# The scan's skip term moves from VectorE to TensorE's accumulation, the sum of squares of the grouped norm to ScalarE

## The chip, the cores and the metric

The kernel runs on one core of a Trainium2 chip. The metric is the device time of the program in microseconds, the median of the runs. The engines are TensorE (PE in the profile; PEld its weight loads), VectorE (DVE), ScalarE (ACT), GpSimd (POOL, which here issues the row gathers) and SyncE (SP, which issues the loads of weights).

## The reference

A decoder layer on 1024 tokens of width 1024. One projection gives the inputs of a pooling mixer, of a Mamba-2 mixer and of two gates; the gated sum goes through an output projection and a LayerNorm, then through a retrieval over 16384 experts and another LayerNorm. The part that matters here is the Mamba-2 mixer:

```python
def ssm_mixer(z, xbc, dt_raw, conv_w, conv_b, dt_bias, a_log, d_skip, norm_w, out_w):
    xbc = jax.nn.silu(causal_depthwise_conv(xbc, conv_w, conv_b))
    ...
    y = ssd_scan(xs, dt, a, bm, cm)
    y = y + d_skip.astype(jnp.float32)[:, None] * xs.astype(jnp.float32)
    y = y.reshape(b, l, SSM_INNER) * jax.nn.silu(z.astype(jnp.float32))
    yg = y.reshape(b, l, SSM_GROUPS, SSM_NORM_GROUP)
    yg = yg * lax.rsqrt(jnp.mean(yg * yg, axis=-1, keepdims=True) + RMS_EPS)
    y = (yg.reshape(b, l, SSM_INNER) * norm_w.astype(jnp.float32)).astype(z.dtype)
    return y @ out_w
```

There are 32 heads of 64 channels in 8 groups of 4 heads (256 channels), a state of 128, and chunks of 128 tokens. The retrieval takes for each token the 128 best of the experts (8 heads, 16 each), a dot product of the token with each expert's row `expert_u[i]`, and a weighted sum of the rows `expert_v[i]`.

## The kernel before

Tokens lie on the 128 partitions for the retrieval; one *pair* is one expert of each of 128 tokens: a gather of 128 rows of 4 KB from `eu` and one from `ev` (for the last 224 of the 1024 pairs one gather of both). VectorE does the dot product (L1498) and, for a part of the pairs, the weighted sum (L1524); the other pairs are summed by TensorE, with a diagonal that ScalarE makes (L929, L621). The rows go through 12 buffers.

The layer ahead of the retrieval runs in five superchunks c of 1, 1, 2, 2 and 2 chunks of 128 tokens. Each superchunk has a stage A of four blocks j (512 channels of x, 2 groups each), then the output pairs (`front_pair`), the output projection with LayerNorm (`front_w`) and the queries and top 16 (`front_d`). The retrieval of the tokens of superchunk c runs beside the layer of superchunk c + 1. Nothing schedules that at run time: every engine has its instructions in an order written out by hand, where `until(p)` puts in the pairs up to number p, and `weave(p, front, steps)` spreads the steps of a generator (each ends at a `yield`) over the pairs up to p. In a block j the scan takes the places 20 to 32 of 32. WIDTHS says how many pairs go with stage A: in superchunk 0 none, in 1 ten a block, in 2 twenty-two, in 3 thirty-one, in 4 thirty-two. While superchunk 0 runs there are no gathers. In superchunks 0 to 2 VectorE does the causal convolution (L1269, L1271), in 3 and 4 TensorE does (L606).

In a block, TensorE projects seven blocks of weights (`front_a1`, L541, L549), turns x, B and C (`front_a2`), and then does the scan steps s, two for each chunk (gg is the group): `scan_scores` (L574, L577) gives the decays' exponents, ScalarE exponentiates them (`decays`, L1037), VectorE multiplies them with C B (`scan_pre`, L1299, signal `m_done`), and `scan_outputs` makes in the bank `ybank` the part from the old state (L589, right half) and the part from the chunk (L592, left half), and in `stbank` the new state's part (L596). The scores of step s + 1 stand before the outputs of step s, and block 7 of the weights (L549) after the outputs of step 0. From step 2 on, the outputs wait for `st_used`, VectorE's state sum of the step before (L1322).

VectorE's `scan_post` then takes the skip product d_skip x (L1310), waits for the outputs (`y_ready`), scales them (L1314), decays the state (L1317), adds the left half (L1320), adds the state's part (L1322), and after a `yield` adds the skip product (L1325), multiplies by silu(z) (L1330) and sums the squares (L1332). After the last step `rms_scale` makes mean + eps (L1338, `rms_in`), ScalarE takes the root (L1051), VectorE the reciprocal (L1341) and ScalarE scales y (L1055), on which TensorE turns y after the first two blocks of weights of the next block j (L709).

## Time and profile before

| what | value |
|---|---|
| time, median of 3 runs | 3943.45 us (3943.39 to 3955.12) |
| span of the profiled execution | 3897.3 us |
| its own time less its span, taken by the median | 46.2 us |
| TensorE busy | 3100.4 us, 80% |
| VectorE busy | 3040.1 us, 78% |
| ScalarE busy | 948.3 us, 24% |
| GpSimd busy | 2136.5 us, 55% |
| gathers and loads | 1394.76 MB, 358 GB/s in the mean |

The profile is one execution. Busy time is the time in which an engine worked on an instruction; issuing and waiting are not in it. The span goes from the first instruction to the last; what a run's time has beyond it lies before and after. In the rows below, a timeline has a start, a duration, the engine, the line of the kernel, the operation, what it writes and reads, and in brackets the engine's idle time just before, with what ended it. A matrix product in float32 has two instructions. "Granted clock" is the share of TensorE's full clock.

### The profile page before, as it was taken

The numbers are of one execution on the slowest core, as the hardware profiler recorded it, in microseconds if no ns is written. First come the engines' busy times: TensorE is split into PE (matmuls) and PEld (weight loads), VectorE is DVE, ScalarE is ACT, GpSimd is POOL, SyncE is SP. The second block draws the span as 40 slices with busy tenths as digits, with TensorE's granted clock in tenths as the row PEclk, the third lists the DMA queues.
The fourth block names the chain that finished last, engine by engine and source line by source line (L and its number), as shares of the span: only waits on it lengthen the run. The fifth ranks groups of instructions, "written<-read, shape, count | busy, mean of one in ns | idle before, by whom it ended". The sixth has DMA issues, their size and how long they took to land.

```text
span 3897.3 us, 43102 instructions
## 1 busy us (share of the span) xinstructions
PE 3100.4 (80%) x13336; PEld 2246.3 (58%) x13336; DVE 3040.1 (78%) x8238; ACT 948.3 (24%) x2282; POOL 2136.5 (55%) x1839
## 2 busy tenths in 40 slices
PE   8983888878789788999998879989878875565665
PEld 8873776567677456777775427777665422121221
DVE  4438975999985799888877988888877986677667
ACT  4411432123321213334312114333312110011111
POOL 0004543465554567766656677676656677555553
PEclk9997988989899999999999899999989897787877
DMA  6668999899888999999999999999999899999997
GB/s 240 210 230 304 377 363 352 319 347 353 312 330 334 335 357 363 400 383 385 381 410 380 351 356 405 379 389 362 375 386 392 305 351 352 423 423 422 424 423 332
DMA packets 316564, 1394.76 MB, mean 358 GB/s; under 512 B 35376, under 2 KB 40880, under 8 KB 251824
## 3 DMA queue, kind: packets, MB, share of 16 engines
q0 software_dynamic: 262656, 1073.86, 71.5%
q1 hardware_dynamic: 52384, 313.43, 20.6%
q10 hardware_dynamic: 1296, 4.72, 0.3%
q8 instruction: 108, 1.77, 0.2%
q14 instruction: 120, 0.98, 0.1%
HBM read 1387.67 MB, written 4.19 MB: 357 GB/s over the span
## 4 chain that ended last, share of the span: by engine, by line
DMA 15%; PE 15%; DVE 11%; POOL 7%; issue 6%; DVEq 2%; ACT 1%; another core or an unknown queue 0%; ACTq 0%; POOLq 0%
PE main L541 6%; POOL rowbuf L501 5%; DMA rowbuf<-euv,idx 4%; DVE rowbuf L1498 3%; DMA rowbuf<-ev,idx 3%; DVE acc L1524 2%; DMA ring<-euv,idx 2%; DMA xT<-euv,idx 2%; PE vbank L621 2%; PE turn L606 2%; DMA rowbuf<-eu,idx 2%; DMA late<-euv,idx 2%; PE main L549 1%; PE main L744 1%; DVE late L1464 1%
## 5 line engine op out<-in xcount | busy, mean ns | idle before, releaser
L501 POOL DMA_INDIRECT rowbuf<-eu,idx x800 | 964.5, 1206 | 989.8 <-DVE hdot L1498 520.8
L1498 DVE CUSTOM_DVE_ANT_0 rowbuf<-rowbuf,hb 128x1024 f32<-128x1024 f32 x884 | 1077.5, 1220 | 175.1 <-DMA rowbuf<-eu,idx 79.4
L501 POOL DMA_INDIRECT rowbuf<-ev,idx x800 | 885.5, 1107 | 453.9 <-issue 217.7
L621 PE MATMUL vbank<-rowbuf,vdiag 128*128 128x512 f32 x1436 | 770.8, 674 | 273.4 <-DMA rowbuf<-ev,idx 191.3
L541 PE MATMUL main<-xT,ring 128*128 128x256 f32 (+1 forms) x4480 | 810.4, 342 | 59.5 <-ACT mm L973 49.0
L541 PEld LDWEIGHTS main<-xT,ring 128*128 128x128 f32 x4480 | 729.2, 195 | 138.0 <-issue 67.0
L1524 DVE SCALAR_TENSOR_TENSOR acc<-rowbuf,hact,acc 128x1024 f32<-128x1024 f32 x525 | 674.8, 1285 | 85.6 <-DMA rowbuf<-ev,idx 63.4
L621 PEld LDWEIGHTS vbank<-rowbuf,vdiag 128*128 128x128 f32 x1436 | 284.3, 212 | 684.7 <-issue 531.5
L929 ACT ACTIVATE vdiag<-ident,hact 128x128 f32<-128x128 f32 x441 | 160.2, 395 | 464.1 <-DVE hact L1507 339.1
L729 PE MATMUL main<-late,ring 128*128 128x256 f32 (+1 forms) x1280 | 235.8, 347 | 32.9 <-issue 23.5
L729 PEld LDWEIGHTS main<-late,ring 128*128 128x128 f32 x1280 | 210.0, 198 | 58.1 <-issue 27.1
L541 PE MATMUL main<-early,ring 128*128 128x256 f32 (+1 forms) x1280 | 231.7, 340 | 0.7 <-ACT early L1099 0.7
L549 PE MATMUL main<-ring,xT 128*128 128x256 f32 x1024 | 228.9, 380 | 2.2 <-issue 2.1
L541 PEld LDWEIGHTS main<-early,ring 128*128 128x128 f32 x1280 | 207.9, 194 | 36.6 <-issue 16.8
L549 PEld LDWEIGHTS main<-ring,xT 128*128 128x128 f32 x1024 | 194.0, 190 | 29.9 <-issue 4.0
L1464 DVE SCALAR_TENSOR_TENSOR late<-iota,late,merged 128x50 f32<-128x50 f32 x1024 | 206.3, 265 | 1.2
L516 POOL DMA_INDIRECT rowbuf<-euv,idx x84 | 107.5, 1280 | 97.5 <-DVE acc L1524 75.8
L744 PE MATMUL main<-ring,merged 128*128 128x256 f32 x512 | 117.1, 390 | 29.5 <-DVE merged L1362 29.5
L621 PE MATMUL vbank<-ring,vdiag 128*128 128x512 f32 x128 | 85.9, 818 | 66.4 <-ACT vdiag L929 64.0
L589 PE MATMUL ybank<-state,CT 128*128 128x256 f32 x128 | 49.0, 470 | 100.9 <-issue 93.2
L744 PEld LDWEIGHTS main<-ring,merged 128*128 128x128 f32 x512 | 100.1, 196 | 47.4 <-DVE merged L1362 31.1
L1360 DVE TENSOR_TENSOR mm<-mm,lexp 128x512 f32<-128x512 f32 (+1 forms) x20 | 11.6, 582 | 145.4 <-ACT mm L1080 145.4
(223 smaller groups left out, 3667.2 us busy)
## 6 DMA issues: line engine op xcount, KB each, us to landing
ring<-wblocks SPq DMA_DIRECT2D x280, 1024.0 KB
rowbuf<-eu,idx POOLq DMA_INDIRECT x800
rowbuf<-ev,idx POOLq DMA_INDIRECT x800
pw<-poolw SPq DMA_DIRECT2D x20, 256.0 KB
h_out<-acc ACTq DMA_DIRECT2D x8, 512.0 KB
xT<-xt SPq DMA_DIRECT2D x3, 1024.0 KB, 17.0
zy<-x SPq DMA_DIRECT2D x3, 1024.0 KB
craw_ln<-ln1g SPq DMA_DIRECT2D x5, 512.0 KB
```

The source lines that it names most:

```text
L501: pool.indirect_dma_start(rows[r], None, (eu, ev)[table], bass.IndirectOffsetOnAxis(ap=idx[c % 2][:, u, k:k + 1], axis=0)).then_inc(row_re ...
L516: pool.indirect_dma_start(both[r], None, euv, bass.IndirectOffsetOnAxis(ap=idx[c % 2][:, u, k:k + 1], axis=0)).then_inc(both_ready[r], 16)
L541: last = pe.matmul(dst_[:, ct * tc:(ct + 1) * tc], w[:, k, ct * P:(ct + 1) * P], src[:, k, 0:tc], start=(k == 0), stop=(k == KD - 1))
L549: last = pe.matmul(dst_[:, t * 256:(t + 1) * 256], src[:, k, t * P:(t + 1) * P], w[:, k, :], start=(k == 0), stop=(k == KD - 1))
L606: last = pe.matmul(dst_[:, ct * tc:(ct + 1) * tc], cdiag[:, ct, k, :], craw[:, n % 2, ct, k:k + tc], start=(k == 0), stop=(k == TAPS - 1))
L621: last = pe.matmul(vbank[half][:, :], vdiag[:, n % DIAGS, :], r[:, half * 512:(half + 1) * 512], start=first, stop=False, skip_group_check ...
L729: last = pe.matmul(dst_[:, ct * tc:(ct + 1) * tc], (lo, hi)[k // KD][:, k % KD, ct * P:(ct + 1) * P], yT[:, k, 0:tc], start=(k == 0), stop ...
L744: last = pe.matmul(dst_[:, n * 256:(n + 1) * 256], merged[:, k, t * P:(t + 1) * P], w[:, k, :], start=(k == 0), stop=(k == KD - 1))
L929: act.activation(vdiag[:, n % DIAGS, :], ident[:, :], ACT.Copy, scale=hact[:, g % 2, q % TOPK:q % TOPK + 1]).then_inc(vdiag_ready, 1)
L1464: dve.scalar_tensor_tensor(out=sel1[:, k, :], in0=iota[:, :], scalar=posf[:, u, k:k + 1], in1=candi[:, u, :], op0=ALU.is_equal, op1=ALU.mu ...
L1498: last = dve.tensor_tensor_reduce(r, r, hb[c % 2][:, t, :], 1.0, 0.0, ALU.mult, ALU.add, hdot[:, g % 2, k:k + 1])
L1524: dve.scalar_tensor_tensor(out=a, in0=r, scalar=hact[:, g % 2, k:k + 1], in1=a, op0=ALU.mult, op1=ALU.add).then_inc(row_free, 1)
```

## The change

The skip term is no longer computed by VectorE. ScalarE makes, once a block j, four diagonal matrices 128x128 (`ddiag`) from the identity and a column of d_skip, now laid out by channel (`dsk`, 128x16). In `scan_outputs` TensorE multiplies x, as it stands by channels (`xs`), with two of them, into the left half of `ybank`. The bank is now one accumulation group: the first product starts it, and the skip products and the four products of the heads add to it. L1310 and L1325 go.

The squares are summed by ScalarE: an activation `Square` with the sum as a second output, one a scan step, its elements written to a part of `yT` that is free at the time. VectorE signals each gate product (`gated`). The root takes mean and eps as its scale and bias, so L1338 goes too.

```diff
+        dsk = sb("dsk", [P, INNER // P])
+        ddiag = sb("ddiag", [P, 4, P])
+        eps = sb("eps", [P, 1])
...
+                if s == 0:
+                    pe.wait_ge(ddiag_ready, c * AJ + j + 1)
                 pe.matmul(ybank[:, GW:2 * GW], CT[:, gg, t * P:(t + 1) * P],
-                          state[:, ds(j * 2 * GW + gg * GW, GW)], start=True, stop=True)
+                          state[:, ds(j * 2 * GW + gg * GW, GW)], start=True, stop=False, skip_group_check=True)
+                for ct in range(2):
+                    pe.matmul(ybank[:, ct * P:(ct + 1) * P], xs[:, 2 * gg + ct, t * P:(t + 1) * P],
+                              ddiag[:, 2 * gg + ct, :], start=False, stop=False, skip_group_check=True)
                 for h in range(HG):
                     last = pe.matmul(ybank[:, h * HD:(h + 1) * HD], mm[:, s % 2, h, :],
-                                     xd[:, s % 2, h * HD:(h + 1) * HD], start=True, stop=True)
+                                     xd[:, s % 2, h * HD:(h + 1) * HD], start=False, stop=(h == HG - 1),
+                                     skip_group_check=True)
...
                 conv_weights(c, j, 3)
+                for ct in range(4):
+                    last = act.activation(ddiag[:, ct, :], ident[:, :], ACT.Copy, scale=dsk[:, ds(j * 4 + ct, 1)])
+                last.then_inc(ddiag_ready, 1)
                 until(o(18))
...
                 until(o(30))
-                act.wait_ge(rms_in, c * AJ + j + 1)
-                act.activation(rms[:, 0:steps], rms[:, 0:steps], ACT.Sqrt).then_inc(rms_sqrt, 1)
+                for s in range(steps):
+                    act.wait_ge(gated, scans(c, j, s) + 1)
+                    act.activation(yT[:, j * 4 + s, 0:GW], yg[:, s // 2, (s % 2) * GW:(s % 2 + 1) * GW], ACT.Square,
+                                   accum_out=rms[:, s:s + 1])
+                act.drain()
+                act.activation(rms[:, 0:steps], rms[:, 0:steps], ACT.Sqrt, bias=eps[:, :], scale=1.0 / GW
+                               ).then_inc(rms_sqrt, 1)
...
                 dve.drain()
-                dve.tensor_tensor(yt2[:, :].rearrange("p (h d) -> p h d", h=HG), xv,
-                                  spread(dsk[:, ds(j * 2 * HG + gg * HG, HG)], HD), ALU.mult)
...
-                dve.tensor_tensor(yt1[:, :], yt1[:, :], yt2[:, :], ALU.add)
-                dve.drain()
...
-                dve.tensor_tensor(y, yt1[:, :], zs[:, t, gg * GW:(gg + 1) * GW], ALU.mult)
-                dve.drain()
-                dve.tensor_tensor_reduce(yt2[:, :], y, y, 1.0, 0.0, ALU.mult, ALU.add, rms[:, s:s + 1])
+                dve.tensor_tensor(y, yt1[:, :], zs[:, t, gg * GW:(gg + 1) * GW], ALU.mult).then_inc(gated, 1)
...
             def rms_scale(c, j):
-                dve.drain()
                 steps = 2 * CHUNK[c]
-                dve.tensor_scalar(rms[:, 0:steps], rms[:, 0:steps], 1.0 / GW, EPS, ALU.mult, ALU.add).then_inc(rms_in, 1)
                 yield
```

Three places in the engines' orders, all in superchunk 2. TensorE at the outputs of the last scan step of a block, before; `scr` is `xd`, `late` and `early` hold yT and x:

```order
L596 MATMUL stbank<-scr,btok 128x256 [waits st_used]
L589 MATMUL ybank<-state,CT 128x256 [waits st_used,y_free,m_done]
L592 MATMUL ybank<-scr,mm 128x64 x4
L596 MATMUL stbank<-scr,btok 128x256 [waits st_used]
L541 MATMUL main<-xT,ring 128x256 [waits main_free,w_ready0]
```

and now:

```order
L606 MATMUL stbank<-scr,btok 128x256 [waits st_used]
L595 MATMUL ybank<-state,CT 128x256 [waits st_used,y_free,m_done]
L598 MATMUL ybank<-ddiag,early 128x128 x2
L601 MATMUL ybank<-scr,mm 128x64 x4
L606 MATMUL stbank<-scr,btok 128x256 [waits st_used]
L545 MATMUL main<-xT,ring 128x256 [waits main_free,w_ready0]
```

Between the product with the state and those of the heads stand two more, with the diagonals (`early` holds `xs`).

VectorE from the last step's outputs to the reciprocal of the norm, before:

```order
L1320 TENSOR_TENSOR yt<-yt,ybank 128x256
L1322 TENSOR_TENSOR state<-state,stbank 128x256 [waits st_ready]
L1325 TENSOR_TENSOR yt<-yt 128x256
L1330 TENSOR_TENSOR zy<-yt,zy 128x256
L1332 ISA yt,rms<-zy 128x256
L1332 ISA rms 128x1
L1498 ISA rowbuf,hdot<-rowbuf,hb 128x1024 [waits row_ready6]
L1498 ISA hdot 128x1
L1524 SCALAR_TENSOR_TENSOR acc<-rowbuf,hact,acc 128x1024 [waits row_ready7,row_free]
L1338 TENSOR_SCALAR rms<-rms 128x4
L1341 RECIPROCAL rmsr<-rms 128x4 [waits rms_sqrt]
```

and now:

```order
L1332 TENSOR_TENSOR state<-state,cdec 128x256
L1335 TENSOR_TENSOR yt<-yt,ybank 128x256
L1337 TENSOR_TENSOR state<-state,stbank 128x256 [waits st_ready]
L1343 TENSOR_TENSOR zy<-yt,zy 128x256
L1507 ISA rowbuf,hdot<-rowbuf,hb 128x1024 [waits row_ready6]
L1507 ISA hdot 128x1
L1533 SCALAR_TENSOR_TENSOR acc<-rowbuf,hact,acc 128x1024 [waits row_ready7,row_free]
L1350 RECIPROCAL rmsr<-rms 128x4 [waits rms_sqrt]
```

The addition, the sum of squares and the scaling are gone; the row products (L1498 and L1524, now L1507 and L1533) stand between the gate product and the reciprocal as they did. The skip product, L1310, stood ahead of L1314 and is gone as well.

ScalarE from the last decays to the scaling of y (`zy` holds yg), before:

```order
L1037 ACTIVATE lexp<-main,nacum 128x128 [waits m_done,l_ready]
L1037 ACTIVATE lexp<-main,nacum 128x128 x3
L1051 ACT_TABLE_LOAD
L1051 ACTIVATE rms<-rms 128x4 [waits rms_in]
L1055 ACTIVATE zy<-zy,rmsr 128x256 [waits rms_rstd]
L1055 ACTIVATE zy<-zy,rmsr 128x256 x3
L973 COPY mm<-main 128x2x256 [waits block_done]
```

and now:

```order
L1050 ACTIVATE lexp<-main,nacum 128x128 [waits m_done,l_ready]
L1050 ACTIVATE lexp<-main,nacum 128x128 x3
L1065 ACTIVATE late,rms<-zy 128x256 [waits gated] x4
L1068 ACT_TABLE_LOAD
L1068 ACTIVATE rms<-rms,eps 128x4
L1073 ACTIVATE zy<-zy,rmsr 128x256 [waits rms_rstd]
L1073 ACTIVATE zy<-zy,rmsr 128x256 x3
L983 COPY mm<-main 128x2x256 [waits block_done]
```

The load of the root's table stood ahead of the wait for `rms_in`; it now stands behind the squares, which wait for `gated`.

## Rows read from the trace of the kernel before

**Rows 1.** Page, part 1: busy time, share of the span, instructions.
```profile
PE 3100.4 (80%) x13336; PEld 2246.3 (58%) x13336; DVE 3040.1 (78%) x8238; ACT 948.3 (24%) x2282; POOL 2136.5 (55%) x1839
```

**Rows 2.** Stretches: columns are in the first line; one block j each.
```profile
core 0: us, PE busy (x) PEld busy (x) DVE busy (x) ACT busy (x) POOL busy (x), PEclk, DMA share, GB/s
98.70:138.40 39.70, 38.84 (x295) 36.14 (x294) 21.23 (x66) 19.39 (x52) 0.00 (x0) 1.00 0.65 220
464.60:512.30 47.70, 41.98 (x290) 38.37 (x290) 43.88 (x94) 21.20 (x54) 25.69 (x21) 0.93 1.01 403
854.20:944.40 90.20, 79.45 (x377) 68.09 (x377) 85.71 (x155) 30.97 (x68) 55.99 (x45) 0.91 0.92 352
1718.00:1824.30 106.30, 100.07 (x467) 82.69 (x466) 90.01 (x147) 43.36 (x106) 71.76 (x62) 0.97 0.99 385
2360.00:2400.00 40.00, 40.00 (x187) 35.15 (x186) 29.51 (x39) 17.98 (x51) 29.80 (x26) 1.00 1.02 413
2457.30:2566.00 108.70, 100.79 (x472) 83.62 (x471) 91.82 (x150) 42.19 (x105) 73.56 (x65) 0.97 1.00 388
1810.90:1817.70 6.80, 4.61 (x14) 3.76 (x15) 6.26 (x16) 0.00 (x0) 4.54 (x4) 0.52 0.97 352
```

**Rows 3.** Timeline, VectorE, superchunk 3; in brackets the idle time before.
```profile
1784.41 0.69 DVE L1299 TENSOR_TENSOR mm<-lexp,cdiag 128x512 f32<-128x512 f32 x1 [2.94 <-ACT lexp L1037]
...
1798.74 0.69 DVE L1299 TENSOR_TENSOR mm<-lexp,cdiag 128x512 f32<-128x512 f32 x1 [1.12 <-ACT lexp L1037]
```

**Rows 4.** Timelines, TensorE, superchunk 2 (first row), then superchunk 3.
```profile
934.97 1.81 PE L592 MATMUL ybank<-scr,mm 128*128 128x64 f32 x8
...
1782.14 1.05 PE L577 MATMUL main<-upper,adtc 128*128 128x128 f32 x8
1783.03 1.02 PE L574 MATMUL main<-mask,ident 128*128 128x512 f32 x2
...
1813.10 1.19 PE L589 MATMUL ybank<-state,CT 128*128 128x256 f32 x2 [5.60 <-issue]
...
1819.05 13.11 PE L541 MATMUL main<-xT,ring 128*128 128x256 f32 x60
```

**Rows 5.** Timeline, VectorE, last scan steps of a block of superchunk 2.
```profile
933.80 0.41 DVE L1322 TENSOR_TENSOR state<-state,stbank 128x256 f32<-128x256 f32 x1
...
934.30 0.42 DVE L1325 TENSOR_TENSOR yt<-yt 128x256 f32<-128x256 f32 x1
...
935.69 1.22 DVE L1498 CUSTOM_DVE_ANT_0 rowbuf<-rowbuf,hb 128x1024 f32<-128x1024 f32 x1
...
938.21 0.42 DVE L1310 TENSOR_TENSOR yt<-early,dsk 128x256 f32<-128x256 f32 x1
938.55 0.42 DVE L1314 TENSOR_TENSOR yt<-ybank,eacum 128x256 f32<-128x256 f32 x1
...
944.12 0.17 DVE L1338 TENSOR_SCALAR rms<-rms 128x4 f32<-128x4 f32 x1
944.57 0.18 DVE L1341 RECIPROCAL rmsr<-rms 128x4 f32<-128x4 f32 x1 [0.27 <-ACT rms L1051]
```

**Rows 6.** Line L577: duration in ns, min/median/max, first and last start.
```profile
L577 PE MATMUL main<-upper,adtc x512: 272/275/421, 46.0 to 2764.6; 128*128 128x128 f32 x171
```

**Rows 7.** Timelines, ScalarE, superchunk 2, then eight diagonals of superchunk 4.
```profile
899.13 0.60 ACT L1000 ACTIVATE zy<-main 128x512 f32<-128x512 f32 x1 [3.75 <-PE main L549]
...
903.58 1.28 ACT L1037 ACT_TABLE_LOAD   x1
904.94 1.15 ACT L1037 ACTIVATE lexp<-main,nacum 128x128 f32<-128x128 f32 x4
...
944.33 0.20 ACT L1051 ACTIVATE rms<-rms 128x4 f32<-128x4 f32 x1 [20.79 <-DVE rms L1338]
944.78 1.71 ACT L1055 ACTIVATE zy<-zy,rmsr 128x256 f32<-128x256 f32 x4 [0.25 <-DVE rmsr L1341]
...
2716.84 2.44 ACT L884 ACTIVATE cdiag<-ident,cw 128x128 f32<-128x128 f32 x8
```

12 lines of the change are left out of this document (7 added, 5 removed).

## The prediction

> **What bounds the kernel now.** I read the page first: VectorE is busy 78% of the span and TensorE 80% [rows 1], so neither bounds the whole, and I went on by stage. The table of stretches has one row for one block j of each kind of superchunk [rows 2]. The block of superchunk 0 belongs to TensorE (38.84 of 39.70 us busy, VectorE 21.23). In superchunk 1 VectorE is busy 43.88 of 47.70 us while the DMA engines stand at share 1.01. In superchunk 2 it is VectorE: 85.71 of 90.20 us, and I take the rest for drains, since its timeline goes from one instruction to the next. In superchunks 3 and 4 it is TensorE: 100.07 of 106.30 us and 100.79 of 108.70. So time saved on VectorE counts fully in four of the twenty blocks and is bounded by something else in the others.
>
> In a block of superchunk 3 the two wait for each other. VectorE waits 2.94 us for the first decay product and 1.12 us for the third, both times for ScalarE's exponentials, which wait for TensorE's scores [rows 3]. TensorE waits once, 5.60 us before the outputs of the last scan step [rows 4], for the state that VectorE adds one step earlier. In the 6.8 us around the end of that wait its granted clock is 0.52 [rows 2], the lower of its two levels (1.2 of 2.4 GHz), and it leaves the scan 5.95 us after the wait.
>
> **What leaves VectorE.** In the timeline of superchunk 2 the skip product (L1310) starts 0.34 us before the next product (L1314) [rows 5]. From L1325 to the instruction behind the sum of squares is 935.69 - 934.30 = 1.39 us; of these three only the gate product stays, 0.35 us by the same spacing, so 1.04 us go. That is 0.34 + 1.04 = 1.38 us for each scan step. Once a block the scaling of the sums and the wait behind it go too: the reciprocal of superchunk 2 followed at 944.57 on L1338 at 944.12 [rows 5], 0.45 us.
>
> **What comes to TensorE.** Two products 128x128 by 128 columns a step. Nearest row: four of that shape, accumulated, from 1782.14 to 1783.03 [rows 4], 0.22 us each, so 0.44 to 0.46 us a step at the full clock (I take 0.46), and about 0.92 at the low one. Bounds: their whole recorded time, as if nothing overlapped, is four instructions (a product is two) of 275 ns [rows 6], 1.1 us a step; and it is 0 where TensorE waits anyway.
>
> **What comes to ScalarE.** Four diagonals a block: eight of the kind last 2.44 us [rows 7], so 1.2 us. They stand ahead of silu(z), before which ScalarE is idle 3.75 us in superchunk 2 [rows 7]: free, and if that cover were gone they would delay the copies of the turned blocks by 1.2 us. TensorE's new wait for them comes after four more steps of ScalarE, so it costs nothing. The squares: one 128x256 activation with a column as scale is 1.71/4 = 0.43 us [rows 7]. All but the last are done while ScalarE waits for the last gate (before, it stood 20.79 us idle there [rows 7]). Behind the last gate stand 0.43 (square), 1.28 (the table load, now after the squares, [rows 7]) and 0.20 (root): 1.9 us. VectorE has in that time, as the order shows, one pair of row products, 938.21 - 935.69 = 2.5 us [rows 5], so it does not wait. Queued behind the squares on ScalarE are the scaling of y and the copy of the pool block. They waited for the same last step before; there the root waited also for the pair of row products, so they start no later now. What the sum's read-out on ScalarE costs no row shows: between 0 and the 0.20 us of its smallest instruction, the root [rows 7]; I take 0, since the cover of 0.6 us holds either.
>
> The trace has a table load at 903.58 of 1.28 us and the exponential that needs it at 904.94 [rows 7], 0.08 us behind its end, so the load costs its own length. The Trainium skill, page "ScalarE: Activation LUTs", section "What ACT_TABLE_LOAD costs", adds a drain of about 1.38 us to each switch. The trace does not agree. By that rule the way behind the last gate would be 3.3 us; a mechanism of that size is rival D.
>
> **The sum by superchunk.**
> - Superchunk 0, four blocks, TensorE bound, two steps each: 8 x 0.46 = +3.7 us. VectorE's saving is worth nothing there.
> - Superchunk 1, four blocks: VectorE would save 2 x 1.38 + 0.45 = 3.2 us of each, but the block moves 403 GB/s x 47.70 us = 19.2 MB, and the fastest that a stretch of mixed traffic shows is 413 GB/s [rows 2]: 46.5 us. So -1.2 us a block: -5 us (0 to -6; without that floor -13).
> - Superchunk 2, four blocks: 4 x 1.38 + 0.45 = 5.97 us less. One new wait: from the state sum of step 2 (start 933.80) VectorE reaches the outputs of step 3 at 938.55 now [rows 5], and 0.34 + 1.04 us sooner then, 937.17; TensorE has them at 934.97 + 1.81 = 936.78 [rows 4], and with the two new products at the low clock at 937.70. So 0.53 us are given back: -5.44 a block, -21.8 us. The DMA floor is far (352 x 90.20 = 31.8 MB, 77 us at 413 GB/s).
> - Superchunks 3 and 4, eight blocks. TensorE's free time in a block is its one wait. What VectorE saves ahead of its third decay product is lost, as that waits for TensorE's scores (1.12 us already [rows 3]), and these come 0.46 later. After it VectorE saves 0.34 + 1.04 (step 1) + 0.34 (head of step 2) = 1.72, so the state for step 3 is there 1.72 - 0.46 = 1.26 us sooner. Then TensorE's way out: 5.95 us now, from 1813.10 to 1819.05 [rows 4]. Of these 4.6 us are at the low clock (to 1817.7 [rows 2]), worth 2.3 at the full one: 3.65 us of work, 4.11 with two more products. If the clock is low as long as now, it is 6.41 us and the block gains 1.26 - 0.46 = 0.8; if it does not fall, 4.11 us and 1.26 + 1.84 = 3.1. The wait shrinks from 5.60 to 5.60 - 3 x 0.46 - 1.26 = 3.0 us, so I take half of the low stretch of 6.8 us, 3.4: 4.11 + 1.7 = 5.81, a gain of 1.26 + 0.14 = 1.4. Eight blocks: -11.2 us (-6 to -25). What the last two steps save behind that point makes VectorE's wait at the next scan longer and nothing else.
>
> Sum: +3.7 - 5 - 21.8 - 11.2 = -34.3 us. The profiled execution has a span of 3897.3 us, so it becomes 3863.0; between a span and the median of 3943.45 lie 46.2 us that the change does not touch. Forecast: 3909.2 us, 0.9% faster. The stages behind the scans (output pairs, query, top 16, the last 224 pairs) keep their length.
>
> **Rivals.** (A) VectorE bounds everywhere from superchunk 1 on: 56 steps x 1.38 + 16 x 0.45 = 84 us less, plus 3.7: 3863 us. Against it: the waits of [rows 3] and the DMA share of 1.01.
> (B) Only superchunk 2 gains. In 3 and 4 VectorE, now faster, waits for rows from the DMA engines (shares 0.99 and 1.00 [rows 2]) and the state comes no sooner; TensorE pays 3 x 0.46 + 0.92 = 2.3 us a block, 18 us, and 3.7 in superchunk 0; superchunk 1 is held by the DMA engines. -21.8 + 18 + 3.7 = 0: 3943 us. For it: the same shares. Against: these are means, and in the scan part of superchunk 3 (1810.90) it is 0.97 at 352 GB/s.
> (C) Slower: the new products cost their whole recorded time, 1.1 us a step, in TensorE's path. Superchunks 0, 3 and 4 have 40 steps there: +44, and 8 of them at the low clock +9; the clock stays low as long as now; the state still comes 1.72 sooner in eight blocks, -14; superchunk 2 gains 5.97 less 1.8 of wait, -17, superchunk 1 -5. Together +17: 3960 us. It decides from about 0.8 us a step. Against it: the spacing of 0.22 us [rows 4], which is steady in a run of such products.
> (D) ScalarE's switch of tables, now behind the last gate, holds the root for as long again as the load itself, 2 x 1.28 us: the root is then 3.2 us behind the gate, against a cover of 2.5, and VectorE waits 0.7 us in each of the eight blocks of superchunks 1 and 2: +5.5, 3914.7 us. No row of this trace shows such a gap. This is the rule of the Trainium skill's page above, whose figure would make it +6.2.
>
> **How the numbers follow.** Forecast 0.64, A 0.07, B 0.13, C 0.08, D 0.08. The forecast's own range is 3892 (superchunk 1 at -6, 2 at -24, 3 and 4 at -25) to 3923 (0, -18, -6). The whole range goes from 3880, which leaves A out, to 3943, which takes in B and leaves out C. A measurement can tell about 0.3%, 12 us, from no change: faster by more is forecast, A, D: 0.79; within 0.3%: B and no more, 0.13; slower: C, 0.08.
>
> **What would show it.** Right: blocks of superchunk 2 at about 85 us instead of 90, with VectorE still without long waits but for half a microsecond at L1329; blocks of superchunk 3 at 104.9 instead of 106.3, with TensorE's wait before the last step's outputs at 3 us and a shorter low clock; VectorE's wait before the first decay product longer; the new products 0.22 us apart; ScalarE's root within 2 us of the last gate. Wrong: blocks of superchunk 0 longer than 40.6 us, VectorE waiting for y in every step, superchunk 3 unchanged or longer (B), or blocks there 5 us shorter (A).

## The result and the profile after

| | before | changed |
|---|---|---|
| median of six executions, us | 3943.4 (3926.2 to 3955.1) | 3909.4 (3898.2 to 3918.9) |
| ratio of the changed kernel to before | | 0.9907 [0.9877, 0.9936] |
| span of the profiled execution, us | 3897.3 | 3910.6 |

The changed kernel is 34.0 us faster, where 34.3 were forecast (3909.2 us). That the sum came out is luck: it hides two large errors that cancel. The stage that was to give most gave little, and the stage that was to give little gave most.

Read the last row of the table first. The time of an execution is its span and about 2 us (1.7 to 2.7 in the runs of this case; 3912.5 for the 3910.6 here). So there never were 46.2 us "between a span and the median": the profiled execution of before took some 3899 us, less than all six timed ones. Other chips ran before in 3879 to 3911 us (medians), and a timed execution can lie 20 us off its median in the kernel before and 26 us in the changed one (36.5 us in a variant below). The profile of the changed kernel is longer than the one of before although its median is lower. Two profiles can't be compared by their spans. They have to be compared piece by piece, and over several executions.

Page of the changed kernel, part 1, beside [rows 1]:

```profile
PE 3133.6 (80%) x13592; PEld 2271.8 (58%) x13592; DVE 2962.0 (76%) x7963; ACT 1002.9 (26%) x2490; POOL 2125.9 (54%) x1839
```

VectorE lost 78 us of work, TensorE got 33, ScalarE 55. Stretches of the changed kernel, with the columns of [rows 2]: one block j each of superchunks 0, 1, 2, 3 and 4, from reciprocal (L1350) to reciprocal; [rows 2] has its counterparts.

```profile
99.90:140.20 40.30, 39.44 (x300) 36.74 (x300) 18.61 (x57) 21.61 (x60) 0.00 (x0) 1.00 0.64 216
459.10:503.50 44.40, 41.01 (x300) 37.75 (x300) 41.26 (x86) 23.52 (x62) 26.62 (x21) 0.96 1.02 413
840.60:930.40 89.80, 82.14 (x401) 70.90 (x400) 80.75 (x139) 34.21 (x80) 55.07 (x45) 0.92 0.94 354
1598.30:1703.60 105.30, 100.01 (x473) 81.60 (x473) 84.17 (x129) 46.32 (x118) 73.81 (x62) 0.98 1.00 392
2454.30:2561.50 107.20, 101.95 (x485) 84.94 (x484) 86.90 (x133) 45.14 (x117) 72.57 (x62) 0.97 0.99 383
```

Superchunk 0 is 0.6 us longer (39.70 to 40.30), superchunk 1 is 3.3 shorter (47.70 to 44.40), superchunk 2 is 0.4 shorter (90.20 to 89.80) although VectorE works 5.0 us less in it. The stretch of superchunk 3 is that superchunk's first block here and its second in [rows 2]; first against first it is 1.3 shorter (106.6 to 105.3), while the second one is 3.3 longer here (106.3 to 109.6).

The whole span in pieces, each the time between two such reciprocals in a trace, means over two profiles of before and three of the changed kernel (two of them from the runs below, on other chips):

```
piece                                   before    changed   difference
start and first block                     61.5       59.8         -1.7
superchunk 0, next three blocks          118.2      120.9         +2.7
turn to superchunk 1, its first block    239.0      233.3         -5.7
superchunk 1, next three blocks          144.1      136.0         -8.1
turn to superchunk 2, its first block    294.0      290.4         -3.5
superchunk 2, next three blocks          283.4      280.5         -2.9
turn to superchunk 3, its first block    475.9      474.3         -1.5
superchunk 3, next three blocks          319.7      321.9         +2.2
turn to superchunk 4, its first block    524.7      519.5         -5.2
superchunk 4, next three blocks          337.4      333.3         -4.1
what stands behind the scans            1109.5     1108.6         -0.9
```

Superchunk 1 and the turns on both its sides hold 17 of the 29 us. From the second row to the sixth the two profiles of before and the three of the changed kernel don't overlap. From the turn to superchunk 3 on they do: the turn to superchunk 4 took 522.5 and 527.0 us before, and 513.3, 520.7 and 524.5 in the changed kernel. So the first and the last five differences can't be told from chance.

**Superchunk 1.** Here the forecast saw a floor of the DMA engines. TensorE's timelines show another bound. First before, then the changed kernel: the products that turn the normed y of the block before (L709, now L719), and the first 96 products of the projections behind them.

```profile
465.90 0.73 PE L709 MATMUL turn<-ident,zy 128*128 128x128 f32 x4 [2.56 <-ACT zy L1055]
466.42 12.49 PE L541 MATMUL main<-xT,ring 128*128 128x128 f32 x96
```
```profile
461.84 0.60 PE L719 MATMUL turn<-ident,zy 128*128 128x128 f32 x4
462.27 10.88 PE L545 MATMUL main<-xT,ring 128*128 128x128 f32 x96
```

Before, TensorE waited 2.56 us for ScalarE's scaled y, and the 96 products behind the wait took 12.49 us, with a granted clock of 0.87:

```profile
466.40:478.90 12.50, 12.50 (x100) 12.50 (x99) 10.92 (x25) 6.11 (x16) 6.52 (x7) 0.87 1.00 402
```

Now the y is there in time and the same products take 10.88. That is 2.56 + 1.61 = 4.17 us, less 2 x 0.44 for the new products: 3.3 us, which is what this block lost.

Other blocks lost more or less. Over all three blocks and all profiles the mean loss is 2.7 us: the first block lost about 4, the other two about 2. The wait is there in each of the twelve blocks of the four profiles with the old order of work (2.56 or 2.57 us), and in none of the changed kernel's. The low clock isn't always right behind it: in four of the twelve the 96 products took 10.88 us all the same. In three of these, of one profile, it comes later in the block, behind TensorE's wait for the turn of C (3.84 us in one), and the blocks are as long, 47.7 to 48.3 us. In the fourth, the second block of another profile, it comes less: the granted clock is 0.96 over a block of 46.7 us, where its neighbours have 0.90 and 48.9 and 48.8 us. In the changed kernel's first and second blocks it is 0.96 too. So the wait is worth 1.7 us net of the new products in every block, and the clock 1.6 us more in some. What else sets the later blocks is taken up behind the runs with one half each.

The scaled y comes sooner for two reasons. VectorE has less to do ahead of the last gate, and the root hangs on that gate instead of on the scaling (L1338) behind a pair of row products. The second reason in the timelines, before and then now:

```profile
508.65 0.42 DVE L1330 TENSOR_TENSOR zy<-yt,zy 128x256 f32<-128x256 f32 x1
...
512.06 0.17 DVE L1338 TENSOR_SCALAR rms<-rms 128x2 f32<-128x2 f32 x1
512.26 0.20 ACT L1051 ACTIVATE rms<-rms 128x2 f32<-128x2 f32 x1 [6.95 <-DVE rms L1338]
512.70 0.91 ACT L1055 ACTIVATE zy<-zy,rmsr 128x256 f32<-128x256 f32 x2 [0.23 <-DVE rmsr L1341]
```
```profile
501.45 0.42 ACT L1065 ACTIVATE late<-zy 128x256 f32<-128x256 f32 x1 [1.68 <-DVE zy L1343]
...
503.30 0.29 ACT L1068 ACTIVATE rms<-rms,eps 128x2 f32<-128x2 f32 x1
503.86 0.91 ACT L1073 ACTIVATE zy<-zy,rmsr 128x256 f32<-128x256 f32 x2 [0.27 <-DVE rmsr L1350]
```

From the start of the last gate to that of the scaling of y it was 4.05 us (508.65 to 512.70); now it is 2.87 (the gate starts at 500.99).

**Superchunk 2.** VectorE's timeline in the changed kernel (in brackets its idle time before; L1287 is the convolution's first operation, L1317 the decay product, L1329 the outputs):

```profile
861.28 0.62 DVE L1287 TENSOR_SCALAR early<-craw_ln,cw 128x256 f32<-128x256 f32 x2 [3.80 <-issue]
...
909.89 0.69 DVE L1317 TENSOR_TENSOR mm<-lexp,cdiag 128x512 f32<-128x512 f32 x1 [1.36 <-ACT lexp L1050]
...
926.20 0.42 DVE L1329 TENSOR_TENSOR yt<-ybank,eacum 128x256 f32<-128x256 f32 x1 [0.60 <-PE ybank L601]
...
927.88 0.43 DVE L1343 TENSOR_TENSOR zy<-yt,zy 128x256 f32<-128x256 f32 x1
...
930.56 0.17 DVE L1350 RECIPROCAL rmsr<-rms 128x4 f32<-128x4 f32 x1
```

VectorE's idle time in the block is 9.1 us (89.80 - 80.75), where it was 4.5 (90.20 - 85.71, [rows 2]). Before, no wait in it was over 0.8 us. The timeline has one more wait now, 1.08 us ahead of the second convolution, but the second profile of before has that one too (1.03). In the other two profiles of the changed kernel the first wait is shorter (2.40 us in one) and the block takes 88.4 and 88.5 us. Ahead of the 3.80 us ScalarE waits for TensorE's projection:

```profile
860.30 0.59 ACT L903 COPY craw_ln<-main 128x512 f32<-128x512 f32 x1 [5.73 <-PE main L545]
```

### The profile page after: what moved, and what is told of

It reads as the page before. It is cut to its first block, busy times and chain, and to the rows that moved or that the text cites. A ratio compares the mean times of both kernels' runs of the same rounds, so it can differ in the third digit from the quotient of the medians.

```text
span 3910.6 us, 43419 instructions
## 1 busy us (share of the span) xinstructions
PE 3133.6 (80%) x13592; PEld 2271.8 (58%) x13592; DVE 2962.0 (76%) x7963; ACT 1002.9 (26%) x2490; POOL 2125.9 (54%) x1839
## 4 chain that ended last, share of the span: by engine, by line
PE 26%; DMA 17%; DVE 16%; issue 8%; POOL 7%; DVEq 4%; ACT 2%; another core or an unknown queue 0%; ACTq 0%; POOLq 0%
PE main L545 11%; POOL rowbuf L505 6%; DMA rowbuf<-ev,idx 4%; DVE rowbuf L1507 4%; DMA rowbuf<-euv,idx 4%; PE main L553 3%; DVE acc L1533 3%; PE vbank L631 3%; PE turn L616 2%; DMA ring<-euv,idx 2%; DMA xT<-euv,idx 2%; DVE late L1473 2%; PE main L754 2%; PE main L739 2%; DVEq L1415 2%
## 5 line engine op out<-in xcount | busy, mean ns | idle before, releaser
L1507 DVE CUSTOM_DVE_ANT_0 rowbuf<-rowbuf,hb 128x1024 f32<-128x1024 f32 x884 | 1078.5, 1221 | 164.1 <-DMA rowbuf<-eu,idx 78.3
L545 PEld LDWEIGHTS main<-xT,ring 128*128 128x128 f32 x4480 | 721.0, 193 | 150.2 <-issue 80.4
L1533 DVE SCALAR_TENSOR_TENSOR acc<-rowbuf,hact,acc 128x1024 f32<-128x1024 f32 x525 | 675.5, 1287 | 81.9 <-DMA rowbuf<-ev,idx 62.3
L616 PE MATMUL turn<-craw_ln,cdiag 128*128 128x256 f32 x512 | 124.1, 393 | 16.0 <-issue 15.1
```

What stands on the lines that cost most here:

```text
L545: last = pe.matmul(dst_[:, ct * tc:(ct + 1) * tc], w[:, k, ct * P:(ct + 1) * P], src[:, k, 0:tc], start=(k == 0), stop=(k == KD - 1))
L616: last = pe.matmul(dst_[:, ct * tc:(ct + 1) * tc], cdiag[:, ct, k, :], craw[:, n % 2, ct, k:k + tc], start=(k == 0), stop=(k == TAPS - 1))
L1507: last = dve.tensor_tensor_reduce(r, r, hb[c % 2][:, t, :], 1.0, 0.0, ALU.mult, ALU.add, hdot[:, g % 2, k:k + 1])
L1533: dve.scalar_tensor_tensor(out=a, in0=r, scalar=hact[:, g % 2, k:k + 1], in1=a, op0=ALU.mult, op1=ALU.add).then_inc(row_free, 1)
```

## The experiments

My theory after the result: each stage had two bounds of nearly the same length, so what leaves one engine is worth something only until the other one binds. In superchunk 1 a wait of TensorE goes, whoever takes it away; in superchunk 2 TensorE's way through the projections takes the place of VectorE's. The rival: the two halves add up, each in the place where the forecast put it. The expectations were written before each run; some weigh a second question, whether the long blocks of superchunks 3 and 4 belong to the change. The kernels ran on three chips: before had medians of 3911.2, 3903.4 and 3878.8 us on the first, the second and the third. A ratio is always to before on the same chip.

### Each half alone, and without the diagonals

First chip. The changed kernel again:

> The changed kernel once more, for the spread of its profile. Theory 1 (TensorE's way from the last scan step to the third block of weights was as long as VectorE's in superchunk 2, so VectorE's saving there is lost): the blocks of superchunk 2 again last about 90, 102 and 90 us, as before the change. Theory 2 (VectorE asks for rows sooner, and the gathers take the bandwidth from the loads of weights in superchunks 3 and 4, so that TensorE starves): blocks there of over 115 us stand again in this profile, perhaps others. If they were chance, all blocks of superchunks 3 and 4 last 104 to 110 us and the span is 3880 to 3890 us. Median 3905 to 3915 us.

Measured: 3880.2 us, 0.9933 [0.9900, 0.9966]. The blocks of superchunk 2 took 88.4, 100.9 and 90.1 us, about as theory 1 has them. Of those of superchunks 3 and 4 none was over 115 us, but one took 113.3.

The skip term on TensorE, the sums of squares on VectorE as before:

```
-                for s in range(steps):
-                    act.wait_ge(gated, scans(c, j, s) + 1)
-                    act.activation(..., ACT.Square, accum_out=rms[:, s:s + 1])
+                act.wait_ge(gated, c * AJ + j + 1)
...
+                dve.tensor_tensor_reduce(yt2[:, :], y, y, 1.0, 0.0, ALU.mult, ALU.add, rms[:, s:s + 1])
...
+                dve.tensor_scalar(rms[:, 0:steps], rms[:, 0:steps], 1.0 / GW, EPS, ALU.mult, ALU.add).then_inc(gated, 1)
```

The scaling and the root's wait for it are back as well, so this kernel has only VectorE's shorter way ahead of the gate.

> The skip term on TensorE as in the change, the squares back on VectorE. By theory 1 VectorE saves 0.84 us a step instead of 1.38 while TensorE pays the same 0.46: superchunk 1 gains 1.7 us a block instead of 3.3, superchunk 0 loses 0.9, superchunk 2 is the same or up to 1 us a block longer than before: 3925 to 3940 us. If VectorE's time counted as the forecast had it: -21.8 x 0.6 in superchunk 2, 3920 us.

Measured: 3881.7 us, 0.9931 [0.9905, 0.9957].

The sums of squares on ScalarE, the skip term on VectorE as before (against the changed kernel):

```
-                for ct in range(2):
-                    pe.matmul(ybank[:, ct * P:(ct + 1) * P], xs[...], ddiag[:, 2 * gg + ct, :], ...)
...
+                dve.tensor_tensor(yt2[...], xv, spread(dsk[...], HD), ALU.mult)
...
+                dve.tensor_tensor(yt1[:, :], yt1[:, :], yt2[:, :], ALU.add)
```

> The squares on ScalarE as in the change, the skip term back on VectorE. TensorE pays nothing: superchunk 0 as before (39.4 us a block), superchunk 1 shorter by 1.5 to 2 us a block. By theory 1 superchunk 2 gains 1 to 2 us a block, as the way to TensorE's outputs does not grow: 3920 to 3932 us. If the two halves of the change add up, this and skip_only together give the -34 us of the change.

Measured: 3885.3 us, 0.9928 [0.9906, 0.9949].

Each half alone gives as much as both together on this chip, as far as the intervals (8 to 13 us to either side) can tell. Both gave more than expected: 29.5 and 26.0 us under before, where the expectations, counted from 3943.4, have 3 to 18 and 11 to 23. The two gains don't add: together they would be 55 us, and both halves in one kernel gave 31. The place where they overlap is the start of superchunk 1's blocks. TensorE's timeline with the skip half alone, then with the norm half alone:

```profile
458.94 0.66 PE L719 MATMUL turn<-ident,zy 128*128 128x128 f32 x4
459.44 10.88 PE L545 MATMUL main<-xT,ring 128*128 128x128 f32 x96
```
```profile
463.99 0.66 PE L711 MATMUL turn<-ident,zy 128*128 128x128 f32 x4 [0.88 <-ACT zy L1062]
464.48 10.88 PE L543 MATMUL main<-xT,ring 128*128 128x128 f32 x96
```

Either half takes the wait from 2.56 us to 0.88 or nothing in all three blocks, and behind it the products take 10.88 us in both. The blocks are 45.5, 45.1, 46.6 us and 45.3, 45.0, 46.6, against 44.3, 45.9, 46.5 with both halves and 48.1, 47.8, 47.9 before. Whichever half comes second finds no wait left to remove.

A rival stands untested here. Once the wait is gone, the DMA engines move 411 to 415 GB/s at share 1.02 in the blocks of superchunk 1 of every variant (one block of the skip half apart, 407 at 1.01), whatever else the kernel does; before they moved 394 to 408. So the blocks may now be held by the DMA engines, their lengths (43.6 to 49.7 us) by how many bytes fall into each, and that too would hide the second half. No run took bytes out of superchunk 1.

The third kernel takes the diagonals and their products away, and puts nothing in their place:

```
-                for ct in range(2):
-                    pe.matmul(ybank[:, ct * P:(ct + 1) * P], xs[...], ddiag[:, 2 * gg + ct, :], ...)
...
-                for ct in range(4):
-                    last = act.activation(ddiag[:, ct, :], ident[:, :], ACT.Copy, scale=...)
```

> The changed kernel without the two products with the diagonals, the diagonals themselves and the wait for them (the skip term is left out of what is computed). It gives what TensorE's part costs. By theory 1: superchunk 0 back to 39.4 us a block (-0.9 each), superchunk 2 shorter by 2 to 3 us a block, superchunks 3 and 4 by 1.8 to 2.3: 3880 to 3890 us. By theory 2 the blocks of superchunks 3 and 4 do not get shorter, as they wait for the DMA engines: 3895 us or more. By rival C of the forecast (1.1 us a step): 3860 us.

Measured: 3870.0 us, 0.9887 [0.9858, 0.9915], 10 us under the changed kernel on this chip, which the intervals don't set clear of noise. Superchunk 0 is back at 39.4 us a block, 0.9 less. Superchunk 2 has blocks of 87.8, 101.1 and 89.7 us: even with no product added, and all of VectorE's savings, the 5.97 us a block don't show. They are 0.6 us shorter, 0.2 longer and 0.4 shorter than with the products, where I had expected 2 to 3 us. So it is not the new products that hold superchunk 2.

### What holds superchunk 2

Second chip. Before once more, as a second profile:

> The kernel before once more, for the spread of its profile. Its blocks of superchunks 0 to 2 agree with the first profile within 1 us (39.4; 48; 90.2, 101.7, 90.6 us). If long blocks (over 112 us) in superchunks 3 and 4 belong to the changed kernel alone (theory 2), at most one of six is long here; if they are chance, one to three are.

Measured: 3909.0 us, 0.9996 [0.9970, 1.0022]; blocks of superchunk 2 of 91.3, 102.0 and 90.9 us, of superchunk 1 of 48.9, 46.7 and 48.8. One of the blocks of superchunks 3 and 4 is long, 123.3 us.

Then the changed kernel and before, each with half of the projections' products left out in superchunk 2:

```
+                kd = KD // 2 if c == 2 and src is xT else KD
...
-                    for k in range(KD):
+                    for k in range(kd):
```

> The kernel before, with half of the products over the input left out in superchunk 2 (its projections take half of their depth; what is computed is wrong there by intent of the run), so that TensorE has about 28 us less to do in each of its blocks while VectorE has the same work. Theory 1 says that VectorE had almost no wait there before: its blocks become 86 to 90 us instead of 90.2, 98 to 101 instead of 101.7, 86 to 90 instead of 90.6.

> The changed kernel with the same half of superchunk 2's projections left out. Theory 1 (TensorE's way takes back what VectorE saves in superchunk 2): with TensorE's way short, VectorE's saving of 5 to 6 us a block shows: blocks 5 us shorter than those of light_before, where with the full projections the two kernels were within 1 us. If something else held superchunk 2 (the DMA engines, VectorE's own waits for ScalarE), the two stay within 1.5 us of each other here too.

Measured, one execution each: 3886.0 and 3857.7 us. The second and third block of superchunk 2, before made light, then the changed kernel made light:

```profile
848.00:937.40 89.40, 56.74 (x247) 46.47 (x247) 85.69 (x155) 30.87 (x68) 56.15 (x45) 0.77 0.93 353
937.40:1035.80 98.40, 60.36 (x260) 50.34 (x259) 93.22 (x167) 33.72 (x72) 56.62 (x45) 0.76 0.86 326
```
```profile
838.80:922.60 83.80, 58.49 (x274) 49.28 (x273) 80.51 (x139) 33.98 (x80) 55.72 (x45) 0.80 0.97 380
922.60:1017.10 94.50, 58.86 (x267) 49.58 (x267) 88.19 (x151) 37.02 (x84) 56.46 (x45) 0.78 0.89 336
```

In before, 23 us less of TensorE's work shorten the usual block by 0.8 us (90.2 to 89.4) and the longer third one by 3.3: there VectorE is nearly the only bound. In the changed kernel the same cut brings the block from 89.8 to 83.8, and VectorE's idle time from 9.1 to 3.3 us. Light against light the change gives 5.6, 3.9 and 5.8 us a block, near the 5.44 of the forecast; with the full projections it gives between -0.3 and 1.8 (two profiles of the changed kernel on two chips, against the first of before). So the savings are real and reach the block, as long as TensorE isn't in the way. In the kernel as it is, VectorE and TensorE take turns in a ring (state sum, outputs, gate; then raw projection, copy, convolution), and TensorE's share of that ring was as long as VectorE's.

### The order of the products

Second chip. The diagonals' products ahead of the wait for the decay product and the state instead of behind it, which was to hide them in that wait:

```
+                for ct in range(2):
+                    pe.matmul(..., ddiag[:, 2 * gg + ct, :], start=(ct == 0), stop=False, ...)
                 pe.wait_ge(m_done, n + 3)
                 if s >= 2:
                     pe.wait_ge(st_used, n - 1 + STATE)
```

> The changed kernel, but TensorE does the two products with the diagonals ahead of its wait for the decay product and the state (they start the accumulation; they need neither), so that in the steps where it waits (two of four in superchunks 2 to 4) they lie in the wait. Theory 1: they then cost nothing where TensorE waits; superchunk 0 stays at 40.3 us a block, TensorE's way out of the scan in superchunks 2 to 4 gets 0.5 to 1 us shorter, the wait of VectorE for the last step's outputs (0.6 us in superchunk 2, 1.4 to 1.8 in 3 and 4) goes: 5 to 12 us less than the changed kernel, up to the -18 us of nodiag at the most. If the products' place does not matter: within 3 us of the changed kernel.

Measured: 3879.5 us, 0.9937 [0.9915, 0.9959], no difference from the changed kernel that can be told (0.9933, 0.9907 and 0.9885 on other chips), where 5 to 12 us were expected. Blocks of superchunk 0 are 39.9 us instead of 40.3. In superchunks 2 to 4 the edit didn't do what it was made for. TensorE before the last outputs of a block of superchunk 2:

```profile
921.68 1.22 PE L593 MATMUL ybank<-ddiag,early 128*128 128x128 f32 x4 [5.67 <-DVE yt L1335]
```

The products wait themselves, for VectorE to read the bank they write to (`y_free`, L1335). It does that at 921.21, 0.33 us ahead of the state sum (921.54) that TensorE waited for in the changed kernel. So they never stood in the wait, and this run doesn't tell what hiding them would be worth.

### A mixture, and a shorter ring of rows

Third chip, with the changed kernel as partner:

> The changed kernel once more, as the partner of the other runs of this call. Expected 0.993 to 0.994 of the kernel before, as in the two calls so far (0.9933, 0.9907), and in its profile blocks of 40.3 us in superchunk 0, 44 to 46.5 in superchunk 1, 88 to 102 in superchunk 2, and 105 to 107 in 3 and 4 except for none to two long ones (over 112 us).

Measured: 3838.3 us, 0.9885 [0.9869, 0.9902]. On this chip the change is worth 40 us, more than the expected 0.993 to 0.994; the blocks are as expected.

The mixture, whose main lines against the changed kernel are these:

```
+SKIP = (1, 2)
...
-                for ct in range(2):
+                for ct in range(2 if c in SKIP else 0):
...
+                if c not in SKIP:
+                    dve.tensor_tensor(yt2[...], xv, spread(dskh[...], HD), ALU.mult)
...
+                if c not in SKIP:
+                    dve.tensor_tensor(yt1[:, :], yt1[:, :], yt2[:, :], ALU.add)
```

> The sums of squares stay on ScalarE everywhere; the skip term is on TensorE in superchunks 1 and 2 alone, and in 0, 3 and 4 VectorE multiplies and adds it as before. Theory 1 (the extra products cost only where TensorE's own order bounds the block, and what they free on VectorE is worth something only where VectorE bounds it): blocks of superchunk 0 back from 40.3 to 39.4 us (0.9 times 4 = 3.6 us), superchunk 1 as in the changed kernel (44 to 46.5), superchunk 2 as there (88 to 102), superchunks 3 and 4 within 1 us a block of it: about 4 us under the changed kernel of this call in all, up to 10 if the nodiag run's 10 us came from superchunks 3 and 4 too. Rival (the skip term on VectorE in 3 and 4 puts VectorE back on the path there): 1.4 us a block more, 8 blocks, so 11 less 3.6 = about 8 us above the changed kernel.

Measured: 3859.9 us, 0.9942 [0.9929, 0.9956]: 21.6 us above the changed kernel, where my theory said 4 under it and the rival 8 above. Superchunk 0 did go back to 39.4 us a block. Superchunks 3 and 4 show what the skip term does there. TensorE before the last outputs of a block of superchunk 3, the changed kernel, then the mixture (before: 5.60 us, [rows 4]):

```profile
1688.38 1.19 PE L595 MATMUL ybank<-state,CT 128*128 128x256 f32 x2 [2.84 <-issue]
1689.37 1.06 PE L598 MATMUL ybank<-ddiag,early 128*128 128x128 f32 x4
```
```profile
1693.03 1.19 PE L596 MATMUL ybank<-state,CT 128*128 128x256 f32 x2 [4.78 <-issue]
1694.02 1.81 PE L602 MATMUL ybank<-scr,mm 128*128 128x64 f32 x8
```

The wait is 2 us shorter with the products on TensorE, and the blocks are equally long (105.7 and 105.4 us): the products fill the wait and pay for it. The two profiles differ by 8.8 us. The mixture is 3.7 us longer in the turn to superchunk 1, 3.0 in superchunk 1 (in its last block, of 49.7 us, VectorE waits 1.7 and 1.8 us for rows, and TensorE 3.2 us behind it for a decay product) and 8.2 in the turn to superchunk 4, and 2.7 shorter in superchunk 0; the other pieces are shorter by 3.4 in all. The 8.2 lie within what this turn varies by in the changed kernel itself (513.3 to 524.5). In the turn to superchunk 1 every profile with the skip term on TensorE in superchunk 0 has 232.8 to 234.1 us, and every one with it on VectorE there has 236.5 to 241.3 (the light pair apart: 234.7 and 235.5). The kernel with no skip term at all has 233.5, so it is VectorE's part that the turn feels. Why was not found, and of the 21.6 us more than half are not located at all. My theory, which valued the skip term's move in superchunks 0, 3 and 4 at nothing or less, is refuted on this chip, and the rival's 8 us are too few as well.

The other two kernels hold the gathers to ten row buffers instead of twelve, in the changed kernel and in before:

```
+HELD = 10
...
-                r = n % ROWS
+                r = n % HELD
...
-                    _, _, by_pe, number_ = ORDER[n - ROWS]
+                    _, _, by_pe, number_ = ORDER[n - HELD]
```

> The changed kernel with its expert-row gathers held to a ring of 10 rows instead of 12, everywhere but in the last stage, where pairs of rows are read from all the memory. Theory 1 (the long blocks of superchunks 3 and 4 come from weight loads that queue behind gathers issued in a burst): a smaller ring caps the burst at 10 rows, so no block over 112 us in superchunks 3 and 4, and times that spread less than the changed kernel's 20 to 40 us; for that, waits for rows get longer elsewhere, some 5 to 15 us in the stretches between superchunks, where the gathers bound. Rival (the long blocks don't hang on the gathers' depth): long blocks as before, one or two in six, and only the loss is seen. For superchunk 1: if its gain came from fewer bytes of rows gathered in the block, blocks of 43 to 44.5 us; if from the earlier root alone, 44 to 46.5 as in the changed kernel.

> The kernel before with its gathers held to a ring of 10 rows instead of 12. Theory 1 (superchunk 1's blocks of 48 us were bound by the DMA engines, with 10.5 MB of rows gathered in a block): blocks of superchunk 1 fall below 47 us, since two rows of 0.5 MB fewer can be ahead; superchunk 2 unchanged within 1 us a block. Rival (they were bound by VectorE's chain of reductions before the root and TensorE's wait behind it, whatever the gathers do): 48 us, as before. In both: no block over 112 us in superchunks 3 and 4 if these come from gathers in a burst, one or two in six if not; total within 15 us of the kernel before, either way.

Measured: 3881.7 us, 1.0005 [0.9994, 1.0016], and 3911.3 us, 1.0078 [1.0062, 1.0094]. Two buffers are worth 43 us to the changed kernel and 32 to before, as much as the whole change; I had expected 15 at most. What they buy was not located. A block of superchunk 1 with ten buffers, in before:

```profile
468.80:516.80 48.00, 42.16 (x290) 38.48 (x290) 43.95 (x94) 21.20 (x54) 25.35 (x21) 0.93 1.01 395
```

It is 48.0 us long with the 21 gathers that it had before (x21, [rows 2]), and TensorE's wait for y is 2.56 us again. So the depth of the gathers doesn't set this block, and the rival that named TensorE's wait fits. Fewer bytes were not tried by it, since as many gathers fall into the block as before. In the changed kernel with ten buffers the blocks are 44.2, 47.3 and 47.5 us, the last two above both of the ranges expected, with the DMA engines at 412 to 413 GB/s: the rival of the DMA engines above would fit that too.

### The long blocks

In superchunks 3 and 4 a block is now and then 110 to 128 us long instead of 105 to 109. I first took this for weights that queue behind gathers. The trace says otherwise. A long block of the changed kernel: a stretch of it, then TensorE in that stretch.

```profile
2601.00:2611.00 10.00, 3.89 (x6) 1.48 (x6) 9.53 (x13) 3.12 (x10) 7.60 (x8) 0.50 1.03 409
```
```profile
2601.46 0.58 PE L545 MATMUL main<-xT,ring 128*128 128x256 f32 x1 [0.82 <-issue]
2602.89 0.59 PE L545 MATMUL main<-xT,ring 128*128 128x256 f32 x1 [0.84 <-issue]
2604.31 1.50 PE L545 MATMUL main<-xT,ring 128*128 128x256 f32 x2 [0.84 <-issue]
```

The products come one by one, about 1.4 us apart, and the idle time is put down to "issue": nothing that the profile shows holds them, no transfer of weights either. The DMA engines are at share 1.03 there. I counted such gaps (over 0.6 us before a projection or turn) in six blocks of superchunks 3 and 4 of each of 14 profiles. Of the 62 blocks without one, 60 are 102 to 111 us long, the other two 111.6 and 113.8; of the 22 with one or more, 12 are over 110, up to 128.3 with ten gaps (11.9 us of idle time). They stand in profiles of before (114.2 and 123.3 us) as in those of the changed kernel (113.3, 116.6, 128.3), and in some of either kind there is none. With ten buffers the changed kernel still has two long blocks (113.8 and 113.5), the second with such a gap of 3.2 us, the first without (TensorE is idle there for 2.0 us ahead of a product with a row of the retrieval). So fewer buffers don't take them away, and they don't belong to the change. They are a good part of why profiles differ: of the 61 us between the longest and the shortest of the changed kernel (on two chips), 30 lie in the blocks of superchunks 3 and 4. What delays TensorE's instructions was not tried. I thought of instructions that arrive late, since the profile has two DMA queues of kind "instruction". It doesn't bear that out: from 2595 to 2620 us, which holds all the gaps of that block, one of the two moved two packets (0.02 MB, 0.2% of the engines' time) and the other none. The cause stays open.

## Why the prediction was right, and where it was not

**The total** was right, the parts were not. Forecast by superchunk and measured (the pieces above, a turn counted to the superchunk it leads to; these are differences of means over several chips, and only those of superchunks 1 and 2 are clear of the spread of the profiles):

```
superchunk       0      1      2      3      4   behind
forecast      +3.7   -5.0  -21.8   -5.6   -5.6        0
measured      +1.0  -13.8   -6.4   +0.7   -9.3     -0.9
```

**Superchunk 2, the step that failed.** "I take the rest for drains, since its timeline goes from one instruction to the next" is true of before, and the sum built on it took VectorE for the only bound. That no wait is seen on the busy engine says that it is the last; it doesn't say how late the next one is. TensorE was busy 79.45 of 90.20 us with a granted clock of 0.91, so it was not far. The forecast followed that one step further, for the outputs of the last scan step, and this wait came as computed (0.60 us, forecast 0.53). It didn't follow it round the block, to the convolution that waits for the raw projection (3.80 us) and to the decay product (1.36 us). Of 5.44 us a block, -0.3 to 1.8 remained; the light pair shows 3.9 to 5.8 with that bound removed.

**Superchunk 1, a step that failed the other way: mis-sized, and for a wrong reason.** "The fastest that a stretch of mixed traffic shows is 413 GB/s: 46.5 us" was made a floor. The block took 44.40 us at 413 GB/s, so 18.3 MB crossed instead of 19.2. The rate held (411 to 415 GB/s once the wait was gone), the volume didn't; where the missing bytes went was not followed. A share of 1.01 showed that the DMA engines were busy, not that anyone waited for them. The bound was in the trace of before as a wait of 2.56 us of TensorE, and the forecast had the cause in hand ("there the root waited also for the pair of row products") and gave it no price. The unfloored figure, 3.2 us a block, is near the measured 3.3 (2.7 in the mean) only by accident: by the runs with one half each, it is a wait with its clock that goes, not VectorE's work. The sum had nothing for the turn to superchunk 1 but its first block, 1.2 us; it gave 5.7.

**Superchunk 0** was right: 0.9 us a block (40.3 for 39.4), 0.45 a step. The +1.0 in the table above holds the start as well, which by itself differs by 4 us between the two profiles of before. The new products, at the full clock and then at the low one:

```profile
897.93 0.61 PE L598 MATMUL ybank<-ddiag,early 128*128 128x128 f32 x4
898.37 1.00 PE L601 MATMUL ybank<-scr,mm 128*128 128x64 f32 x8
...
923.50 1.06 PE L598 MATMUL ybank<-ddiag,early 128*128 128x128 f32 x4
924.36 0.95 PE L601 MATMUL ybank<-scr,mm 128*128 128x64 f32 x4
```

The next product follows 0.44 us and 0.86 us behind, as forecast (0.44 to 0.46, 0.92). Rival C, the whole recorded 1.1 us, is out.

**Superchunks 3 and 4**: in the first block of superchunk 3 the wait of TensorE shrank from 5.61 to 2.84 us, in the second from 5.60 to 3.04 in two profiles and 3.55 in the third (forecast 3.0). The blocks without gaps (see the long blocks) have means of 106.3 us before and 105.6 in the changed kernel in superchunk 3, 109.3 and 108.3 in superchunk 4: 0.7 and 1.0 us less, where 1.4 were forecast. With a spread of 102.2 to 107.2 us in the changed kernel's blocks of superchunk 3 that is no clear gain, and the mixture, whose wait is 4.78 us, has blocks as short. So the wait came as forecast; that the blocks gain by it is not shown.

**ScalarE** did what was forecast. The end of a block of superchunk 2, behind the last gate at 927.88:

```profile
928.34 0.42 ACT L1065 ACTIVATE late<-zy 128x256 f32<-128x256 f32 x1 [4.53 <-DVE zy L1343]
928.66 0.19 ACT L1065 ACTIVATION_READ_ACCUMULATOR late<-zy 128x1 f32 x1
928.89 1.28 ACT L1068 ACT_TABLE_LOAD   x1
930.19 0.30 ACT L1068 ACTIVATE rms<-rms,eps 128x4 f32<-128x4 f32 x1
```

The root is done at 930.49, 2.2 us behind the gate's end (forecast 1.9; the read-out of 0.19 and a root of 0.30 instead of 0.20 are the rest), and the reciprocal at 930.56 doesn't wait. The load starts 0.04 us behind the read-out and the root 0.02 behind the load: rival D is out. The Trainium skill, page "ScalarE: Activation LUTs", section "What ACT_TABLE_LOAD costs", adds a drain of about 1.38 us to the switch; the trace shows none here.

**Span and median.** "Between a span and the median lie 46.2 us that the change does not touch" was wrong as a statement: about 2 us lie outside the span, the rest was a profiled execution quicker than the timed ones. As arithmetic it did no harm, since a difference was added to a median.

**Rivals A and B.** A (VectorE bounds everywhere) is refuted by superchunk 2. B (only superchunk 2 gains) had it upside down.

## What to carry to other kernels

Before work is taken from an engine that bounds a stage, measure how late the next one is: follow the ring of waits once round the block, or halve the other engine's work in one run and see whether the saving appears. Look first for a wait of TensorE with slow products behind it; here 2.56 us of waiting cost 4.2 in the block shown, and either of two small steps that removed it gave all of the gain that could be told, so two changes that both remove it don't add. Before a run is read, see in its trace that its edit did what it was made for: products moved ahead of one wait can stand in another. A DMA share of 1.0 over a stretch is no floor by itself, and one profiled execution is no base for sums of 1%: take two, and compare by pieces.

## What the runs showed of the hardware

- A sum over a row on ScalarE is two instructions, the activation of 0.42 us and a read-out of its own of 0.19 us that starts 0.32 us after it.
- The same 96 products of TensorE took 12.26 to 12.51 us behind a wait of 2.56 us in eight blocks of superchunk 1 (granted clock 0.87 over them in the one shown), and 10.88 us behind the same wait in four others; behind a wait of 0.88 us, or none, they took 10.88 in all that were looked up.
- In the blocks of superchunk 1 the DMA engines moved 395 to 408 GB/s at a share of 1.01 and 411 to 415 at 1.02: shares that look alike hide rates that differ by 5%.
- TensorE's instructions can come one by one, 1.4 to 2.2 us apart, for 10 us and more with no wait shown; in the two longest such stretches the DMA engines were at a share of 1.03 and the granted clock was 0.50 and 0.53.
- The gain of one and the same change was measured as 0.67%, 0.93% and 1.15% in three measurements; the intervals of the first and the last touch only just (0.9900 to 0.9966, 0.9869 to 0.9902).
